# Sparse attention in pairs of heads: high and low parts added in the v product, transposes in place of the fold matrix, loads issued by SyncE

## What is computed

```python
proj = h @ w_in
(u_a, z_a, q, k, v, z_b, q_idx, k_idx, w_idx, g_a, g_b) = split(proj)
y_a = multiscale_pool(u_a, w_pool_group, pool_scale) * silu(z_a)
# 8 heads of 64, one shared k and v; q and k normalised, rotated in part
score = sum_h relu(q_idx[h] @ k_idx.T) * w_idx[h]     # causal
keep  = top 256 keys of score for each query
p     = softmax(where(keep, q[h] @ k.T / 8, -inf))
y_b   = (p @ v) * silu(z_b)
merged = sigmoid(g_a) * (y_a @ w_branch_a) + sigmoid(g_b) * (y_b @ w_branch_b)
out = x + gate * (merged @ w_out)
```

## Time and profile before

| | us |
|---|---|
| median of 3 runs | 863.4 |
| lowest and highest | 863.24, 864.71 |
| the profiled execution | 862.37 |
| its span, first to last instruction | 860.4 |

### The profile page before, as it was taken

How to read it: one execution, slowest core, us unless ns; L and a number is a source line. 1 busy time by engine, 2 the same in 40 slices (tenths; PEclk the granted TensorE clock), 3 DMA queues, 4 the chain that set the end, 5 groups by cost and what they waited for, 6 DMA issues and landing times.

```text
span 860.4 us, 14154 instructions
## 1 busy us (share of the span) xinstructions
PE 813.7 (95%) x5038; PEld 715.9 (83%) x5042; DVE 602.5 (70%) x1257; ACT 341.9 (40%) x615; POOL 371.4 (43%) x320
## 2 busy tenths in 40 slices
PE   3899999999999999999999998789999999999998
PEld 3699998889988888887888876678888887889998
DVE  5846448978889889888888454466787895664432
ACT  6463455664212222233422222556667672330000
POOL 1024624434425758835542104788755002792100
PEclk9899999999999999999999998999999999999999
DMA  9930110014422322321042224544321004753332
GB/s 353 357 99 2 50 50 26 13 39 127 130 62 86 99 62 78 94 73 35 27 135 93 91 74 157 168 142 123 123 88 61 14 1 143 248 174 110 111 100 73
DMA packets 62686, 87.96 MB, mean 102 GB/s; under 512 B 5881, under 2 KB 44317, under 8 KB 61726
## 3 DMA queue, kind: packets, MB, share of 16 engines
q10 hardware_dynamic: 28226, 41.96, 14.9%
q1 hardware_dynamic: 32476, 38.86, 14.4%
q0 software_dynamic: 1920, 6.29, 1.9%
HBM read 66.12 MB, written 20.97 MB: 101 GB/s over the span
## 4 chain that ended last, share of the span: by engine, by line
PE 83%; DVE 5%; issue 3%; ACT 2%; DMA 2%; SPq 1%; POOL 1%; POOLq 1%; DVEq 0%; ACTq 0%
PE pp L552 22%; PE pp L553 22%; PE pp L554 22%; PE pp L862 3%; PE ps L689 3%; PE ps L690 3%; PE pt L845 3%; DMA ada_w<-in_w_ada 2%; PE pt L873 1%; DVE pT L1864 1%; DVE logit L1930 1%; PE ps L769 1%; POOLq L1519 1%; SPq L463 1%; ACT qT L1233 0%
## 5 line engine op out<-in xcount | busy, mean ns | idle before, releaser
L495 POOL TENSOR_TENSOR w_lo<-w_raw,w_hi 128x1024 fp32r<-128x1024 f32 x50 | 122.2, 2462 | 215.6 <-ACT w_hi L490 166.5
L1801 DVE TENSOR_SCALAR_CACHE_REDUCE junk<-score,cand 128x384 uint8<-128x384 f32 (+1 forms) x186 | 168.6, 944 | 19.3 <-issue 13.3
L552 PE MATMUL pp<-hT_hi,w_hi 128*128 128x512 f32 x384 | 150.2, 391 | 0.0
L554 PE MATMUL pp<-hT_hi,w_lo 128*128 128x512 f32 x384 | 149.5, 389 | 0.0
L553 PE MATMUL pp<-hT_lo,w_hi 128*128 128x512 f32 x384 | 149.4, 389 | 0.0
L552 PE MATMUL pp<-w_hi,hT_hi 128*128 128x256 f32 x352 | 101.2, 287 | 0.5 <-ACT zb_out L1039 0.5
L554 PE MATMUL pp<-w_hi,hT_lo 128*128 128x256 f32 x352 | 99.4, 282 | 0.0
L553 PE MATMUL pp<-w_lo,hT_hi 128*128 128x256 f32 x352 | 99.4, 282 | 0.0
L552 PEld LDWEIGHTS pp<-hT_hi,w_hi 128*128 128x128 f32 x384 | 72.1, 188 | 16.2 <-issue 0.8
L554 PEld LDWEIGHTS pp<-hT_hi,w_lo 128*128 128x128 f32 x384 | 72.1, 188 | 15.2
L553 PEld LDWEIGHTS pp<-hT_lo,w_hi 128*128 128x128 f32 x384 | 72.1, 188 | 14.5
(11 more groups left out here) (270 smaller groups left out, 1862.3 us busy)
## 6 DMA issues: line engine op xcount, KB each, us to landing
w_raw<-in_w_in SPq DMA_DIRECT2D x36, 512.0 KB, 3.8
ada_w<-in_w_ada SPq DMA_DIRECT2D x7, 1024.0 KB, 11.6
sgb_spill<-stage ACTq DMA_DIRECT2D x16, 256.0 KB, 2.0
sga_spill<-stage ACTq DMA_DIRECT2D x16, 256.0 KB, 2.1
stage<-sga_spill ACTq DMA_DIRECT2D x16, 256.0 KB, 3.1
ma_spill<-stage POOLq DMA_DIRECT2D x16, 256.0 KB, 2.6
gate_w<-in_w_ada ACTq DMA_DIRECT2D x16, 256.0 KB, 2.9
w_raw<-in_w_out SPq DMA_DIRECT2D x8, 512.0 KB, 4.1
```

Source lines behind the costliest of these rows:

```text
L495: nc.gpsimd.tensor_tensor(lo, raw, hi.bitcast(F32), ALU.subtract).then_inc(w_lo_done, 1)
L552: nc.tensor.matmul(o, a_hi, b_hi, start=first, stop=False)
L554: return nc.tensor.matmul(o, a_lo, b_hi, start=False, stop=last)
L1801: v.tensor_scalar(junk[:, n % 2, 0:keys(b)], score[:, score_at(b):score_at(b + 1)], least, None, ALU.is_ge, ALU.add, accum_out=cnt[:, n:n ...
```

## The change

- The transposes of the last mask go from unit 16 to unit 17, its counts from 17 to 18.
- Heads are worked in pairs for the product with v. `pT` holds for each key tile the high parts of two heads and then the low parts. The product takes 256 columns, both heads side by side, first of the high, then of the low parts, and adds both into the same PSUM columns. So the reduction of `output_parts` becomes a copy, once for two heads, at odd steps.
- `fold` is gone. Each group of four heads is turned by four plain transposes of 128x128, and VectorE adds the two halves of v in a reduction over 512 columns that writes y. The scaling by the reciprocal goes to POOL, which multiplies z by it ahead of y times z, with a drain between; the reciprocal gets a second buffer.
- The exponentials are written over the logits, in three buffers `prob` in place of two and two.
- The order within a step changes: TensorE does the logits before the transposes, ScalarE the exponential before the copies, VectorE the logits before the group's outputs and the low part.
- The query rows and their stacked form have one buffer in place of two.
- SyncE issues all loads that ScalarE issued from branch A on: gates, query and z rows, `load_gate`, e, x rows. They stand in SyncE's one order, among the weight pieces. In the last loop over branch B's 16 units the pieces of `w_out` stand behind units 5, 7, 11 (two) and 15 (two), each ahead of the next e load, and the last two pieces ahead of the first x row.

```diff
-    MASK_UNIT = {11 + n: FREE_BLOCKS + n for n in range(NSEL)}
+    MASK_UNIT = {11 + n + (n == NSEL - 1): FREE_BLOCKS + n for n in range(NSEL)}
...
-                q_row=alloc(s, "q_row", [P, 2, H * HD]), z_row=alloc(s, "z_row", [P, 2, H * HD]),
-                q_stk=alloc(s, "q_stk", [P, 2, H, 2 * HD], F32R), qT=alloc(s, "qT", [P, 2, H, P], F32R),
-                logit=alloc(s, "logit", [P, 2, L]), prob=alloc(s, "prob", [P, 2, L]),
-                pT=alloc(s, "pT", [P, 2, NT, 2, P], F32R), oT=alloc(s, "oT", [P, 8, P])),
+                q_row=alloc(s, "q_row", [P, H * HD]), z_row=alloc(s, "z_row", [P, 2, H * HD]),
+                q_stk=alloc(s, "q_stk", [P, H, 2 * HD], F32R), qT=alloc(s, "qT", [P, 2, H, P], F32R),
+                prob=alloc(s, "prob", [P, 3, L]),
+                pT=alloc(s, "pT", [P, 2, NT, 2, 2, P], F32R), oT=alloc(s, "oT", [P, 2, 2, P])),
...
+            first_wa = pieces_through[name_of[("wa", 0)] - 1]
+            for n in range(5, first_wa + 4):
                 load_piece(n)
+            nxt = first_wa + 4
+            for n in range(3):
+                load_sga(n)
+            load_piece(nxt)
+            sp.wait_ge(pp_full, PP_HT)
+            sp.wait_ge(q_spilled, 16 * NT)
+            for i in range(4):
+                sp.wait_ge(zb_spilled[i], 16 * 4)
+            load_q(0)
+            load_z(0)
+            load_z(1)
+            load_sga(3)
+            load_q(1)
+            load_sga(4)
+            load_sga(5)
+            sp.wait_ge(bias_ready, NSEL + 1)
+            sp.dma_start(gate[0:1, :], b_ada[:, 2 * D:3 * D]).then_inc(gate_row_in, 16)
+            for n in range(3):
+                load_gate(n)
+            load_piece(nxt + 1)
+            nxt += 2
+            for i in range(HEADS):
+                if i in WA_STEP:
+                    if WA_STEP[i] < 14:
+                        load_sga(WA_STEP[i] + 2)
+                    if WA_STEP[i] % 4 == 3:
+                        load_piece(nxt)
+                        nxt += 1
+                if i - 2 in GATE_AT and GATE_AT[i - 2] + 3 < 2 * KD:
+                    load_gate(GATE_AT[i - 2] + 3)
+                if i % H == 5 and i // H + 2 < NT:
+                    load_q(i // H + 2)
+                if i % H == 6 and 2 <= i // H + 1 < NT:
+                    load_z(i // H + 1)
+            sp.wait_ge(logit_done, HEADS)
+            sp.wait_ge(ma_full, 16)
+            for i in range(4):
+                sp.wait_ge(ma_out[i], 16 * 4)
+            for n in range(4):
+                load_e(n)
+            for n in range(16):
+                if n in WB_LAST:
+                    for _ in range(1 if WB_LAST[n] < 2 else 2):
+                        load_piece(nxt)
+                        nxt += 1
+                if n + 4 < 16:
+                    load_e(n + 4)
+            sp.wait_ge(m_raw_done, 16)
+            for n in range(4):
+                load_x_row(n)
+            for n in range(4 * NT - 4):
+                if n == NT:
+                    for m in range(nxt, len(pieces)):
+                        load_piece(m)
+                load_x_row(n + 4)
...
             for i in range(HEADS + 6):
+                if i < HEADS:
+                    b, h = i // H, i % H
+                    if h == 0:
+                        pe.wait_ge(pt_free_a, pt_done[pt_at[("qT", b, 1)]][0])
+                    o = ps_claim(("S", i))
+                    two_pass(o, qT[:, b % 2, h, :], kT, keys(b)).then_inc(ps_full, 1)
                 if 0 <= i - 2 < HEADS:
                     j, b = i - 2, (i - 2) // H
                     pe.wait_ge(prob_done, j + 1)
                     for g in range((b + 4) // 4):
                         o = pt_claim(("PT", j, g))
                         for t in range(4 * g, min(4 * g + 4, b + 1)):
-                            last = nc.tensor.transpose(o[:, (t % 4) * P:(t % 4 + 1) * P], prob[:, j % 2, t * P:(t + 1) * P],
+                            last = nc.tensor.transpose(o[:, (t % 4) * P:(t % 4 + 1) * P], prob[:, j % 3, t * P:(t + 1) * P],
                                                        ident[:])
                         last.then_inc(pt_full, 1)
-                if i < HEADS:
-                    b, h = i // H, i % H
-                    if h == 0:
-                        pe.wait_ge(pt_free_a, pt_done[pt_at[("qT", b, 1)]][0])
-                    o = ps_claim(("S", i))
-                    two_pass(o, qT[:, b % 2, h, :], kT, keys(b)).then_inc(ps_full, 1)
                 if i < KA * (16 - WA_FIRST):
                     branch_a(KA * WA_FIRST + i)
-                if 0 <= i - 3 < HEADS:
-                    j, b = i - 3, (i - 3) // H
+                if 0 <= i - 4 < HEADS and i % 2 == 0:
+                    j, b, u = i - 3, (i - 3) // H, (i - 4) // 2
                     wait_done(pe, pt_done[pt_at[("PT", j, b // 4)]], pt_free_a, pt_free_v)
-                    pp_claim(("pv", j))
+                    pp_claim(("pv", u))
 
                     for t in range(b + 1):
-                        last = nc.tensor.matmul(pp[0][:, 0:2 * P], v2[:, t, :],
-                                                pT[:, j % 2, t, :, :].rearrange("p s q -> p (s q)"),
-                                                start=(t == 0), stop=(t == b))
+                        for s in range(2):
+                            last = nc.tensor.matmul(pp[0][:, 0:2 * P], v2[:, t, :],
+                                                    pT[:, u % 2, t, s, :, :].rearrange("p h q -> p (h q)"),
+                                                    start=(t == 0 and s == 0), stop=(t == b and s == 1))
                     last.then_inc(pv_done, 1)
                 if i % H == 4 and i // H + 1 < NT:
                     q_transposes(i // H + 1)
                 if 0 <= i - 4 < HEADS and (i - 4) % 4 == 3:
                     n = (i - 4) // 4
-                    pe.wait_ge(pp_free_v, pp_done[pp_at[("pv", 4 * n + 3)]][1])
+                    pe.wait_ge(pp_free_v, pp_done[pp_at[("pv", 2 * n + 1)]][1])
                     o = pt_claim(("out", n))
                     for h in range(4):
-                        last = nc.tensor.matmul(o[:, h * HD:(h + 1) * HD], oT[:, (4 * n + h) % 8, :], fold[:],
-                                                start=True, stop=True)
+                        last = nc.tensor.transpose(o[:, h * P:(h + 1) * P], oT[:, h // 2, h % 2, :], ident[:])
                     last.then_inc(pt_full, 1)
                 if i in GATE_ROWS:
                     g = GATE_ROWS[i]
...
-            for n in range(3):
-                load_gate(n)
             act.wait_ge(bias_ready, NSEL + 1)
-            act.dma_start(gate[0:1, :], b_ada[:, 2 * D:3 * D]).then_inc(gate_row_in, 16)
             for i in range(HEADS + 6):
+                if 0 <= i - 1 < HEADS:
+                    j, b, h = i - 1, (i - 1) // H, (i - 1) % H
+                    act.wait_ge(logit_done, j + 1)
+                    if h % 4 == 0 and b >= 2:
+                        act.wait_ge(o_sum, 2 * (b - 1))
+                    r = (b % 2) * H + h
+                    nc.scalar.activation(prob[:, j % 3, 0:keys(b)], prob[:, j % 3, 0:keys(b)], ACT.Exp, scale=-1.0,
+                                         bias=neg_max[:, j % 2:j % 2 + 1],
+                                         accum_out=row_sum[:, r:r + 1]).then_inc(prob_done, 1)
                 if 0 <= i - 2 < HEADS:
                     j, b = i - 2, (i - 2) // H
-                    if j >= 2:
-                        act.wait_ge(pv_done, j - 1)
+                    if j >= 4:
+                        act.wait_ge(pv_done, (j - 4) // 2 + 1)
                     for g in range((b + 4) // 4):
                         t0, t1 = 4 * g, min(4 * g + 4, b + 1)
                         o = pt_take(("PT", j, g))
-                        nc.scalar.activation(pT[:, j % 2, t0:t1, 0, :], o[:, 0:(t1 - t0) * P].rearrange(
+                        nc.scalar.activation(pT[:, j // 2 % 2, t0:t1, 0, j % 2, :], o[:, 0:(t1 - t0) * P].rearrange(
                             "p (t q) -> p t q", q=P), ACT.Copy).then_inc(pt_free_a, 1)
...
+                    pool.wait_ge(inv_done, n + 1)
+                    pool.wait_ge(z_in[b % 2], 16 * (b // 2 + 1))
+                    z = z_row[:, b % 2, 4 * f * HD:4 * (f + 1) * HD]
+                    zh = z.rearrange("p (h d) -> p h d", d=HD)
+                    gp.tensor_tensor(zh, zh, row_inv[:, n % 2, :].unsqueeze(2).to_broadcast([P, 4, HD]), ALU.mult)
+                    pool.drain()
                     pool.wait_ge(o_sum, n + 1)
-                    pool.wait_ge(z_in[b % 2], 16 * (b // 2 + 1))
                     y = y_row[:, b, 4 * f * HD:4 * (f + 1) * HD]
-                    gp.tensor_tensor(y, y, z_row[:, b % 2, 4 * f * HD:4 * (f + 1) * HD], ALU.mult).then_inc(y_done, 1)
+                    gp.tensor_tensor(y, y, z, ALU.mult).then_inc(y_done, 1)
...
-            def output_parts(j):
-
-                dve.wait_ge(pv_done, j + 1)
```

(37 more changed lines are left out.)

150 lines of the change are left out of this document (52 added, 98 removed).

## The result

The changed kernel takes 893.6 us (median of 4 runs, 892.4 to 895.2) against 863.3 (862.4 to 864.7) for the kernel before on the same chip: 1.035 of it, 95% interval 1.0329 to 1.0372. It is 30 us slower where I forecast 5 faster, and outside my range.

A forecast was written before the change was run, and what follows sets the result against it. TensorE, busy 95% of the span, was taken as the bound. Terms -6.3 + 3.0 - 2.5 - 4.4 - 1.9 + 6.9 = -5.2 gave 858.2 us on the median; own range 854.5 to 862, overall 851 to 866.5.

The forecast's parts named there:

- Mask: Before the attention loop: moving the last mask removes TensorE's 3.93 us wait and the half clock behind it, -6.3 us.
- Scaling on POOL: Attention loop before step 28: POOL's added multiply and drain per group delay TensorE's query transposes, +3.0 us.
- Loads inside the loop: Attention loop: ScalarE's load waits move to SyncE, with gates, queries and z rows issued no later; counted as 0.
- Transposes for the fold: First six groups, steps 31 to 51: four transposes replace eight fold records, 0.42 us less per group, -2.5 us.
- term 5: Last two attention blocks, steps 47 to 63: less TensorE work and nearly all its idle gone through the new order, -4.4 us.
- term 6: Tail from step 64: with e loads on SyncE the last head's copy starts 1.5 us sooner, plus the fold's 0.42, -1.9 us.
- The output stage: Output stage: x rows leave behind w_out pieces, so TensorE idles 4.7 us and its clock falls, +6.9 us.
- Rival C: Before step 28: each added POOL drain waits out a store, making the kernel slower, 868.6 us; chance 0.13.
- rival A: POOL isn't late and VectorE lets go of the last blocks: 852 us; chance 0.18.

The follow-up runs named there:

- b_mask17_r5: Kernel before with one edit, the last tie mask at unit 17, in six more runs: 856.52 us against 863.23, ratio 0.992.
- a_single_old_xq: Changed kernel with single-head products, old orders on three engines, first query and gate loads and first four x rows ahead of weight pieces: 859.5 us.
- a_single_old: Changed kernel with each head's product by itself and the old orders on TensorE, ScalarE and VectorE: 867.8 us.
- a_single_pe_new: Changed kernel with each head's product by itself, old orders on ScalarE and VectorE, new order on TensorE alone: 869.0 us.
- a_pe_new_pairs: Changed kernel in pairs, old orders on ScalarE and VectorE, only TensorE's order new: 875.8 us.
- a_act_old: Changed kernel in pairs with one edit, ScalarE's old order (copy from PSUM ahead of the exponential): 893.5 us.
- b_mask17: Kernel before with one edit, the last tie mask at unit 17: 856.25 us.
- b_mask17_e: Kernel before with the last tie mask at unit 17 and e loads on SyncE, x rows still on ScalarE: 858.35 us, ratio 0.9948.

## Why the prediction was wrong, point by point

The runs lay the 30.3 us out in a row, each step a difference of two medians or single runs. The price of a step depends on the orders around it, so this row is one path among several, and the +1.2 and +0.1 are not told from nothing:

| from | to | us | what |
|---|---|---|---|
| before 863.3 | b_mask17_r5 856.5 | -6.8 | mask |
| 856.5 | a_single_old_xq 859.5 | +3.0 | scaling, transposes, in-place exponentials, e loads |
| 859.5 | a_single_old 867.8 | +8.3 | query and x rows behind pieces |
| 867.8 | a_single_pe_new 869.0 | +1.2 | TensorE's order |
| 869.0 | a_pe_new_pairs 875.8 | +6.8 | pairs |
| 875.8 | a_act_old 893.5 | +17.7 | VectorE's order |
| 893.5 | after 893.6 | +0.1 | ScalarE's order |

1. **Mask, -6.3:** right, -6.7, with the first logit product at 528.17 in b_mask17_r5 where I had 528.2. In the changed kernel it comes at 530.08. What is late there is not the bias but the counts of the last mask (0.66 us of idle TensorE at 524.85): ScalarE's copy of the mask ends only at 524.56, since ScalarE had stood 5.27 us for the late query load and works in order.
2. **Scaling on POOL, +3.0:** right in kind and, as far as it lies ahead of step 31, in place. Left out, it gives 3.6 back in all and 5.2 by group 6. The split at step 26 ended later than I had it, at 598.0 (started 596.75), and the query transposes followed it only at 601.51, so POOL was not what TensorE waited for at step 28, as I had it. The wait is at step 20 (7.62 us).
3. **Loads inside the loop, 0:** the sentence that SyncE issues queries "no later than now" fails for the first one. I followed the loads inside the loop and not the one in front of it, which was moved past a piece that waits for POOL. It cost 2.8 (a_single_old_xq).
4. **Transposes for the fold, -2.5:** right in kind as far as seen, smaller. Without pairs and new orders, groups 7 to 15 take 102.8 us (a_single_old_xq) against 104.1 (b_mask17): -1.3. In-place exponentials and the scaling on POOL are still in that run, so the transposes by themselves were not priced. I also counted one group twice: six here, four in term 5 and one in term 6 make 17 with the first six. The records are cheaper by about what I took, 9.9 us for 64 against 16.1 for 128 fold products; that the rest goes to the chain of the banks is argued.
5. **The last two blocks, -4.4: the step that failed.** Steps 47 to 63 take 74.1 us instead of 54.8, +19.3. I wrote that the new order "gives exponential, transposes and copy one VectorE step more to finish in" and took nearly all the idle time as gain. I had looked at who gets more time and not at what comes to stand behind the logit: the read-out of the group, which holds one of TensorE's two transpose banks. In these steps VectorE's order makes up 14.7 of the 19.3 (58.7 us in a_pe_new_pairs, 73.4 in a_act_old, group 10 to 14), TensorE's 2.5 (with single products) and the pairs 1.3; over the whole loop it costs 17.7. The other part belongs to no term: I had costed the pairs by the sum of TensorE's work, which stays the same, and put the cover of each single step at nothing. That costs 6.8 over the loop, most of it outside these steps. VectorE's and TensorE's work did shrink as I said; it was not what set the pace once the order had changed.
6. **The tail, -1.9:** groups 14 to 15 are the only stretch behind group 5 that got shorter (11.3 to 10.1). With the mask alone the e loads on SyncE win 0.8 there (b_mask17_e), and at the end the first output tile is later. In the changed kernel VectorE stood 2.7 us for the last e tile, where I had 0.7.
7. **The output stage, +6.9:** right in place and mechanism. TensorE stood 5.09 us behind the second tile, where I had 4.7, and its clock was 0.50 from 801 to 806. From group 15 to the end the kernel is 7.0 longer, but that holds term 6's end and the late e tile; taking the x rows out from behind the pieces gives 5.5 (145.4 to 139.9). The x rows left at 796.51, behind the second piece (SPq L454, 793.28 to 796.47), and VectorE multiplied at 800.33, after standing 6.53 us:

```profile
800.33 0.42 DVE L1980 TENSOR_TENSOR o_row<-pp,gate 128x256 f32<-128x256 f32 x1 [6.53 <-DMA x_row<-in_x]
...
793.28 3.19 SPq L454 DMA_DIRECT2D w_raw<-in_w_out  x2
```

The x row took 3.8 us from its issue behind the pieces, and 2.4 in a_single_old_xq, where it leaves ahead of them (764.61 to 767.01). In b_mask17_e the x rows leave from ScalarE, at 762.08, right beside two pieces of SyncE's (761.52 to 764.71), and the first takes 3.35:

```profile
762.08 1.80 ACTq L1324 DMA_DIRECT2D x_row<-in_x  x4
```

So a row can land nearly as late from a queue of its own while pieces are in flight; the common queue accounts for 0.5 us between these two runs.
The rule of the Trainium skill that I had weighed there ("DMA: Bandwidth & Descriptors", Queues, rings and completion order: one issuer's descriptors are consumed in order) is not contradicted by the 3.8, which lies between my 3.4 and its 4.1, but no run here tests it by itself.

Rival C had the sign and the wrong place (drains on POOL). No rival of mine named VectorE's order, though most of its price could be put together beforehand: a logit of 1.2 us in front of a read-out, eight groups. In rival A the bound of term 5 gives 1.6 over the forecast and not 1.2, which changes nothing. That the change reordered three in-order queues should have been a rival of its own, on the slower side.

What stays open: why TensorE's new order is worth 7.8 us in pairs and nothing with single products was not taken apart (its waits for the read-out fall, from 8.7 to 2.6 us), and how the +3.0 of the second row divides was not tried apart from the scaling; by the marks all of it lies ahead of group 4 (579.50 in b_mask17_r5, 584.68 in a_single_old_xq), where TensorE's wait for the query split at step 20 is 1.70 and 6.16 us.
